# Moving eight weight buffers by 64 bytes within a 128-byte line of on-chip memory, in a float32 transformer kernel

## The chip, the core and the metric

The kernel runs on one core of one Trainium2 chip. The metric is the device time of one execution in microseconds (us). TensorE is the matmul engine (PE in the profile, and PEld for its loads of the stationary operand), VectorE is DVE, ScalarE is ACT, GpSimd is POOL, and SyncE is SP, which issues the DMAs. SBUF is the on-chip memory from which the engines read (128 partitions; an address here is a byte offset within a partition, the same in all of them), and PSUM is the memory that TensorE writes.

## The reference, cut to what matters

Two residual-network blocks run after one another over 256 tokens of width 1024: projections, a gated convolution, memory attention, stick-breaking attention, gated linear attention, spatial gating, and three gated feed-forward networks. Nearly all the work is in products of the form

```python
h = rmsnorm(x, gain)                                   # (256, 1024)
p = h @ w                                              # every projection, w is (1024, n)
x = x + (act(h @ w_gate) * (h @ w_up)) @ w_down        # three times, 2816 wide
```

All inputs and outputs are float32, and the products are asked for at float32 accuracy.

## The kernel before, in words

**Weights.** The weights are cut into 356 slots of 128 x 1024 float32 (512 KB each), which pass through the kernel in one fixed order (`STAGES`, line 41). With 48 more pieces for the modulation vectors they form one stream of 404 loads. SP loads them one after another into six buffers `raw0` to `raw5` (line 350), and waits before each load until the buffer's last reader is done (line 349).

**Halves.** TensorE reads a faster float32 format (fp32r) that holds fewer bits, so each weight is split into a high and a low part, and so is each activation. For slot n, ACT copies `raw` into `w_hi[n % 4]` in that format (line 886), and DVE subtracts: `w_lo[n % 4] = raw - w_hi[n % 4]` (line 1408; in the third feed-forward network POOL does about every second one, line 2108). Four buffers of each kind form the ring (`RING = 4`). ACT waits at line 885 until TensorE has used the slot four earlier.

**Matmuls.** A product is made of three: high x high, high x low and low x high (`mm3`, lines 378 to 381). A call `pe.matmul(o, w, x)` loads `w` as the stationary operand, 128 columns that stay in the array (the profile shows this as LDWEIGHTS), and streams `x`, the moving operand, past it. The load for the next matmul runs while the present one streams. There are two kinds of slot:
- `tall` (line 390) and `down` (line 519): 8 chunks x 3 matmuls. Stationary is a 128-column chunk of `w_hi` or `w_lo`; moving are 256 tokens of an activation (`H`, `Y`, `CX`, `HP`, or `G` in `down`). 24 matmuls a slot.
- `wide` (line 401), called for the value projections by `project_tokens`: the other way round. Stationary are 128 tokens of an activation, moving are 512 or 256 columns of `w_hi` or `w_lo`.

```python
def mm3(o, wh, wl, xh, xl, start, stop):                                              # 378
    pe.matmul(o, wh, xh, start=start, stop=False, skip_group_check=True)              # 379
    pe.matmul(o, wh, xl, start=False, stop=False, skip_group_check=True)              # 380
    return pe.matmul(o, wl, xh, start=False, stop=stop, skip_group_check=True)        # 381
```

Products that are not of weights (attention, sums over partitions, transposes) go through `mm` (line 384) as plain float32 and read no weight half.

**Order.** Each engine has a program written out by hand (`pe_program`, `act_program`, `dve_program`, `pool_program`, `sync_program`). Side tasks such as attention are put between slots by generators (`Side`, `Pace`). The engines meet only at semaphores (`mark`, `past`).

**Places in SBUF.** `sb(...)` allocates tensors in the order of the calls from line 214 on, each start rounded up to 32 bytes. The compiled program of before has them at these places:

| tensors | first start (bytes) | start modulo 128 |
|---|---|---|
| `raw0` to `raw5` | 1152 | 0 |
| `w_hi0` to `w_hi3` | 25728 | 0 |
| `w_lo0` to `w_lo3` | 42112 | 0 |
| `X`, `H_hi`, `H_lo`, `Y_hi`, `Y_lo`, `SQ`, `RS` | 58496 | 0 |
| `G_hi0` to `G_lo1`, `GF`, `consts` | 109696 | 0 |
| `CROW` | 120992 | 32 |
| `ARENA` and its areas of whole kilobytes | 129472 | 64 |
| `CX_lo`, `CX_hi` (activations of the context) | 191424 | 64 |
| `HP` (rows of 258 elements) | 207808 | 64, and 8 bytes on for each chunk |

A chunk of a weight half is 512 bytes long and one of `H`, `Y` or `CX` 1024 bytes, so every chunk of one tensor begins at the same place modulo 128. The one exception is `HP`, whose chunks are 1032 bytes apart.

Of the kernel before, what the change touches and what calls it, by code (L numbers as in the profile page):

```python
# [8 lines left out]
P = 128  # L9
# [17 lines left out]
STACK = 96  # L27
EPS = 1e-6
RING = 4
RAW = 6  # L30

F32 = mybir.dt.float32
# [3 lines left out]
ALU = mybir.AluOpType  # L36
AX = mybir.AxisListType.X

# [15 lines left out]
for _l, _j in ((_l, _j) for _l in range(2) for _j in range(FC)):  # L54
# [4 lines left out]
    MOD_ORDER += _now  # L59
    MODS_AFTER[AT[f"ffn{_l}"] + (RING + 1 + 2 * _j if _j < 2 else RING + 3 * _j)] = _now  # L60
assert MOD_ORDER == list(range(NMOD))
# [17 lines left out]
def raw_of(kind, n):  # L79
    return LOAD_OF[kind, n] % RAW  # L80

# [42 lines left out]
class Signals:  # L124
# [14 lines left out]
    def mark(self, name, *index, by=1):  # L139
        sem = SEMAPHORE.get(name, name)  # L140
        self.count[sem] = self.count.get(sem, 0) + by
        assert (name, *index) not in self.value, (name, index)
        self.value[(name, *index)] = self.count[sem]
        return self.sem(name), by

    def past(self, name, *index):
        return self.sem(name), self.table[(name, *index)] if self.table else 1
# [43 lines left out]
def lo_by(n):  # L191
    first = AT["ffn2"] + RING
    return "lo_pool" if n >= first and (n % 2 or n == first) else "lo_dve"
# [6 lines left out]
def freed(i):  # L200
    kind, n = LOADS[i]
    return (lo_by(n), n) if kind == "slot" else ("mod_dot", n, 0)


def build(nc, table, stream, vec, xT, memT, ctxT, c_rows, sq_consts, masks, scan_mask, sgu_bc, sgu_wT, gla_w2, out):
    pe, act, dve, pool, sp = nc.tensor, nc.scalar, nc.vector, nc.gpsimd, nc.sync
    with ExitStack() as ctx:
        def sb(name, shape, dt=F32):
            return ctx.enter_context(nc.sbuf_tensor(name, shape, dt))
# [2 lines left out]
        mark, past = signals.mark, signals.past  # L212

        raw = [sb(f"raw{r}", [P, D]) for r in range(RAW)]
        w_hi = [sb(f"w_hi{r}", [P, D], F32R) for r in range(RING)]
        w_lo = [sb(f"w_lo{r}", [P, D], F32R) for r in range(RING)]
        X = sb("X", [P, KC, T])
        H = (sb("H_hi", [P, KC, T], F32R), sb("H_lo", [P, KC, T], F32R))
        Y = (sb("Y_hi", [P, KC, T], F32R), sb("Y_lo", [P, KC, T], F32R))
# [123 lines left out]
        def sync_program():  # L343
# [3 lines left out]
            for i, (kind, n) in enumerate(LOADS):  # L347
                if i >= RAW:
                    sp.wait_ge(*past(*freed(i - RAW)))
                sp.dma_start(raw[i % RAW][:], stream[i]).then_inc(*mark(f"loaded{i % RAW}", kind, n, by=16))  # L350
                if (kind, n) == ("slot", 0):
                    sp.dma_start(MEM[:, 4:8], memT[:, 4:8]).then_inc(*mark("mem_half1", by=16))
                if (kind, n) == ("slot", 1):
                    sp.dma_start(X[:], xT).then_inc(*mark("x_in", by=16))
                if (kind, n) == ("slot", AT["a_c"]):
# [13 lines left out]
        def pe_program():  # L369
# [16 lines left out]
            def slot():  # L386
                pe.wait_ge(*past(lo_by(n), n))
                return n % RING

# [482 lines left out]
        def act_program():  # L872
# [5 lines left out]
            def fill():  # L878
                nonlocal n
                if n >= N_SLOTS:  # L880
                    return
                at = raw_of("slot", n)
                act.wait_ge(*past(f"loaded{at}", "slot", n))
                if n >= RING:
                    act.wait_ge(*past("used", n - RING))
                act.activation(w_hi[n % RING][:], raw[at][:], ACT.Copy).then_inc(*mark("hi", n))  # L886
                n += 1

            def squares(tag, src, ready, at=SQ):
                for c in range(0, KC, 2):  # L890
                    if ready:
                        act.wait_ge(*past(*ready[c // 2]))
                    act.activation(at[:, c:c + 2], src[:, c:c + 2], ACT.Square).then_inc(*mark("sq", tag, c // 2))
# [103 lines left out]
            def residual_square(l, into=None, g=None):  # L997
                def then(i):
                    act.wait_ge(*past("added", l, i))
                    act.activation(SQ[:, i], X[:, i], ACT.Square).then_inc(*mark("res_sq", l, i))  # L1000
                    if into is not None:
                        act.activation(into[0][:, i, 0:T], X[:, i], ACT.Copy,
                                       scale=g(i)).then_inc(*mark("h_hi", l, i))
# [77 lines left out]
            def block1_end():  # L1081
                pace = Pace()
                squares("final", X, [("x_add", 1, c) for c in range(KC // 2)])
                yield from pace.to(4)
# [141 lines left out]
            act.wait_ge(*past("x_in"))  # L1226
            squares("mix0", X, None, CSQ)
            fill()
# [1072 lines left out]
```

## Time and profile before

| | |
|---|---|
| three runs | 1151.97, 1153.01 and 1153.58 us; median 1153.01 |
| the profiled execution | 1151.95 us, of which the span from the first to the last instruction is 1150.6 us |
| granted TensorE clock | 0.995 of full speed |
| DMA | 221.49 MB, mean 192 GB/s |

A row of the profile names the source line, the engine, the operation, the output and inputs (buffer numbers left out), the shape, and the count. After the bar stand the busy time in us and the mean duration of one in ns, and after a second bar the engine's idle time ahead of these instructions, with what ended most of it. Matmuls overlap, so the duration of one is not the pace: the pace is read from start to start. The busy share of PE says little for the same reason.

### The profile page before, as it was taken

To read this page: it belongs to the slowest core of one execution; us is meant where nothing else is said; L and a number is where in the kernel's file an instruction comes from. 1 tells how busy PE (TensorE), PEld (TensorE's weight loads), DVE (VectorE), ACT (ScalarE), POOL (GpSimd) and SP (SyncE) were. 2 spreads that over 40 slices of the span, in tenths; PEclk is the share of its full clock that TensorE was granted. 3 is DMA by queue.
4 is the path that set the end of the run, shared out by engine and by line. 5 is a ranking of instruction groups with operands and counts; after the bars stand their busy time and mean duration, and the time that the engine had idled before them with its cause. 6 is when DMAs were issued, how large, how long until landed. Compare 5 with 4: busy or idle time off the path is not lost.

```text
span 1150.6 us, 21726 instructions
## 1 busy us (share of the span) xinstructions
PE 1124.2 (98%) x8918; PEld 1085.8 (94%) x8918; DVE 837.2 (73%) x1304; ACT 627.7 (55%) x951; POOL 146.2 (13%) x109
## 2 busy tenths in 40 slices
PE   7999999999999999999999999999999998999997
PEld 6989999999998899999999888989999998999996
DVE  5767687888876766777777677497646788767766
ACT  5655644434665655444444675676547465455553
POOL 0002201000000003000000000000000044344441
PEclk9999999999999999999999999999999999999999
DMA  8655578776644345788888655354435544555640
GB/s 324 220 160 171 177 234 282 240 252 208 200 132 150 125 140 191 247 272 276 270 263 285 235 165 183 110 183 155 140 123 172 183 165 129 192 182 177 191 158 37
DMA packets 60322, 221.49 MB, mean 192 GB/s; under 512 B 6720, under 2 KB 6976, under 8 KB 59840
## 3 DMA queue, kind: packets, MB, share of 16 engines
q1 hardware_dynamic: 59760, 218.53, 58.5%
q8 instruction: 71, 1.16, 0.4%
q10 hardware_dynamic: 288, 1.05, 0.2%
q0 software_dynamic: 176, 0.52, 0.1%
q14 instruction: 27, 0.22, 0.1%
HBM read 219.03 MB, written 1.05 MB: 191 GB/s over the span
## 4 chain that ended last, share of the span: by engine, by line
PE 83%; DVE 11%; ACT 4%; issue 2%; DMA 1%; SPq 0%; ACTq 0%; DVEq 0%
PE PS L379 23%; PE PS L380 23%; PE PS L381 23%; PE PS L384 13%; DVE w_lo L1408 3%; ACT w_hi L886 2%; DVE PS L2053 2%; DVE ARENA L1441 1%; DMA ARENA<-memT 1%; DVE SQ L1441 0%; DVE SQ L1716 0%; DVE H_lo L1451 0%; ACT ARENA L983 0%; DVE Y_lo L1451 0%; DVE Y_lo L1447 0%
## 5 line engine op out<-in xcount | busy, mean ns | idle before, releaser
L1408 DVE TENSOR_TENSOR w_lo<-raw,w_hi 128x1024 fp32r<-128x1024 f32 x324 | 396.9, 1228 | 164.6 <-ACT w_hi L886 164.0
L886 ACT ACTIVATE w_hi<-raw 128x1024 fp32r<-128x1024 f32 x356 | 371.6, 1054 | 133.4 <-PE PS L381 107.6
L379 PE MATMUL PS<-Y_hi,w_hi 128*128 128x256 f32 x1208 | 347.0, 287 | 9.5 <-DVE Y_lo L1447 3.4
L380 PE MATMUL PS<-Y_lo,w_hi 128*128 128x256 f32 x1208 | 343.0, 284 | 0.0
L381 PE MATMUL PS<-Y_hi,w_lo 128*128 128x256 f32 x1208 | 342.9, 284 | 0.0
L379 PEld LDWEIGHTS PS<-Y_hi,w_hi 128*128 128x128 f32 x1208 | 232.6, 193 | 13.7 <-issue 4.3
L380 PEld LDWEIGHTS PS<-Y_lo,w_hi 128*128 128x128 f32 x1208 | 232.8, 193 | 0.5 <-issue 0.2
L381 PEld LDWEIGHTS PS<-Y_hi,w_lo 128*128 128x128 f32 x1208 | 232.8, 193 | 0.0
L379 PE MATMUL PS<-H_hi,w_hi 128*128 128x256 f32 x768 | 220.1, 287 | 1.7 <-DVE w_lo L1408 0.9
L380 PE MATMUL PS<-H_lo,w_hi 128*128 128x256 f32 x768 | 217.3, 283 | 0.0
L381 PE MATMUL PS<-H_hi,w_lo 128*128 128x256 f32 x768 | 217.2, 283 | 0.0
L379 PEld LDWEIGHTS PS<-H_hi,w_hi 128*128 128x128 f32 x768 | 147.1, 192 | 6.4 <-issue 3.0
L379 PE MATMUL PS<-G_hi,w_hi 128*128 128x256 f32 x528 | 149.6, 283 | 1.9 <-DVE G_lo L1539 1.9
L380 PE MATMUL PS<-G_lo,w_hi 128*128 128x256 f32 x528 | 149.4, 283 | 0.0
L381 PE MATMUL PS<-G_hi,w_lo 128*128 128x256 f32 x528 | 149.4, 283 | 0.0
L380 PEld LDWEIGHTS PS<-H_lo,w_hi 128*128 128x128 f32 x768 | 147.2, 192 | 0.1
L381 PEld LDWEIGHTS PS<-H_hi,w_lo 128*128 128x128 f32 x768 | 147.2, 192 | 0.0
L379 PEld LDWEIGHTS PS<-G_hi,w_hi 128*128 128x128 f32 x528 | 101.4, 192 | 2.3 <-issue 2.3
L380 PEld LDWEIGHTS PS<-G_lo,w_hi 128*128 128x128 f32 x528 | 101.4, 192 | 0.0
L381 PEld LDWEIGHTS PS<-G_hi,w_lo 128*128 128x128 f32 x528 | 101.4, 192 | 0.0
L1028 ACT ACTIVATE GF<-GF 128x256 f32<-128x256 f32 x44 | 18.4, 418 | 140.0 <-DVE GF L1550 140.0
L2108 POOL TENSOR_TENSOR w_lo<-raw,w_hi 128x1024 fp32r<-128x1024 f32 x32 | 77.8, 2433 | 113.0 <-ACT w_hi L886 113.0
(251 smaller groups left out, 1392.1 us busy)
## 6 DMA issues: line engine op xcount, KB each, us to landing
raw<-stream SPq DMA_DIRECT2D x404, 512.0 KB, 4.1
ARENA<-memT SPq DMA_DIRECT2D x2, 512.0 KB, 7.6
X<-xT SPq DMA_DIRECT2D x1, 1024.0 KB, 11.2
ARENA<-ctxT SPq DMA_DIRECT2D x1, 1024.0 KB, 5.3
ARENA<-memT SPq DMA_DIRECT2D x1, 1024.0 KB, 9.4
outT<-ARENA SPq DMA_DIRECT2D x2, 512.0 KB, 2.6
CROW<-c_rows SPq DMA_DIRECT2D x1, 512.0 KB, 10.2
ARENA<-c_rows SPq DMA_DIRECT2D x1, 512.0 KB, 12.3
```

Of the source, the lines that this page charges most:

```text
L379: pe.matmul(o, wh, xh, start=start, stop=False, skip_group_check=True)
L380: pe.matmul(o, wh, xl, start=False, stop=False, skip_group_check=True)
L381: return pe.matmul(o, wl, xh, start=False, stop=stop, skip_group_check=True)
L384: return pe.matmul(o, w, x, start=start, stop=stop, skip_group_check=True)
L886: act.activation(w_hi[n % RING][:], raw[at][:], ACT.Copy).then_inc(*mark("hi", n))
L1028: act.activation(GF[:], GF[:], ACT.Silu).then_inc(*mark("silu", l, j))
L1408: dve.tensor_tensor(w_lo[n % RING][:], raw[raw_of("slot", n)][:], w_hi[n % RING][:], ALU.subtract).then_inc(*mark("lo_dve", n))
L1441: dve.scalar_tensor_tensor(via[:, c], src[:, c], g(c), rs[1], ALU.mult, ALU.mult).then_inc(*mark("norm", tag, c))
L2053: dve.scalar_tensor_tensor(conv_sum(j), IMGS[:, j % 2, r0:r0 + ROWS, c0:c0 + COLS], gain("fconv", j + t * FC), conv_sum(j), ALU.mult, ALU. ...
L2108: pool.tensor_tensor(w_lo[n % RING][:], raw[raw_of("slot", n)][:], w_hi[n % RING][:], ALU.subtract).then_inc(*mark("lo_pool", n))
```

## The change

Two unused tensors of 16 float32 a partition (64 bytes) are allocated: one ahead of the weight halves, one behind them. The eight weight halves so begin 64 bytes later (25792 and 42176, modulo 128: 64), and everything behind them 128 bytes later, at the same place modulo 128 as before. The raw buffers lie ahead of both and do not move. No instruction is added, removed or reordered.

```diff
+HALF_LINE = 16
 ...
         raw = [sb(f"raw{r}", [P, D]) for r in range(RAW)]
+        sb("phase", [P, HALF_LINE])
         w_hi = [sb(f"w_hi{r}", [P, D], F32R) for r in range(RING)]
         w_lo = [sb(f"w_lo{r}", [P, D], F32R) for r in range(RING)]
+        sb("whole", [P, HALF_LINE])
         X = sb("X", [P, KC, T])
```

## Rows read from the trace of the kernel before

**Rows 1.** The page: busy time, share of the span, instructions of each engine
```profile
PE 1124.2 (98%) x8918; PEld 1085.8 (94%) x8918; DVE 837.2 (73%) x1304; ACT 627.7 (55%) x951; POOL 146.2 (13%) x109
```

**Rows 2.** The page: the chain of waits that ended last, by engine
```profile
PE 83%; DVE 11%; ACT 4%; issue 2%; DMA 1%; SPq 0%; ACTq 0%; DVEq 0%
```

**Rows 3.** Groups by line and shape: matmuls with a weight half, tall kinds
```profile
L379 PE MATMUL PS<-Y_hi,w_hi 128*128 128x256 f32 x1208 | 347.0, 287 | 9.5 <-DVE Y_lo L1447 3.4 <-DVE w_lo L1408 3.2 <-DVE G_lo L1539 2.7
...
L379 PE MATMUL PS<-H_hi,w_hi 128*128 128x256 f32 x768 | 220.1, 287 | 1.7 <-DVE w_lo L1408 0.9 <-DVE H_lo L1626 0.2
...
L379 PE MATMUL PS<-G_hi,w_hi 128*128 128x256 f32 x528 | 149.6, 283 | 1.9 <-DVE G_lo L1539 1.9
...
L379 PE MATMUL PS<-CX_hi,w_hi 128*128 128x256 f32 x40 | 11.5, 287 | 0.0
...
L379 PE MATMUL PS<-HP,w_hi 128*128 128x258 f32 x32 | 9.4, 292 | 0.0
```

**Rows 4.** Stretches: us, each engine's busy time (instructions), granted clock, DMA share, GB/s
```profile
870.00:939.00 69.00, 69.00 (x578) 69.00 (x577) 54.69 (x80) 39.11 (x55) 7.96 (x6) 1.00 0.59 189
1000.00:1120.00 120.00, 120.00 (x1002) 120.00 (x1001) 88.15 (x160) 61.40 (x98) 50.48 (x21) 1.00 0.57 181
460.00:640.00 180.00, 180.00 (x1503) 180.00 (x1502) 135.18 (x198) 80.06 (x109) 15.77 (x22) 1.00 0.83 270
...
140.00:305.00 165.00, 164.62 (x1373) 164.44 (x1372) 134.11 (x208) 77.36 (x111) 13.55 (x19) 1.00 0.75 238
```

**Rows 5.** PE in order of time (start, duration), tall slot with CX, 14 matmuls
```profile
412.33 0.28 PE L380 MATMUL PS<-CX_lo,w_hi 128*128 128x256 f32 x1
...
413.86 0.28 PE L381 MATMUL PS<-CX_hi,w_lo 128*128 128x256 f32 x1
```

**Rows 6.** PE in order of time, tall slot with Y just begun, 13 matmuls
```profile
668.16 0.28 PE L379 MATMUL PS<-Y_hi,w_hi 128*128 128x256 f32 x1
...
669.58 0.28 PE L379 MATMUL PS<-Y_hi,w_hi 128*128 128x256 f32 x1
```

**Rows 7.** PE in order of time, wide slot with Y: first, 7th, 24th matmul
```profile
751.95 0.40 PE L384 MATMUL PS<-w_hi,Y_hi 128*128 128x512 f32 x1
...
753.34 0.39 PE L384 MATMUL PS<-w_hi,Y_hi 128*128 128x512 f32 x1
...
757.19 0.39 PE L384 MATMUL PS<-w_lo,Y_hi 128*128 128x512 f32 x1
```

**Rows 8.** PE in order of time, wide slot with CX, 13 matmuls
```profile
645.10 0.39 PE L384 MATMUL PS<-w_hi,CX_hi 128*128 128x512 f32 x1
...
647.90 0.39 PE L384 MATMUL PS<-w_hi,CX_hi 128*128 128x512 f32 x1
```

**Rows 9.** PE in order of time, slot with HP (258 moving columns), 21 matmuls
```profile
939.46 0.28 PE L379 MATMUL PS<-HP,w_hi 128*128 128x258 f32 x1
...
941.86 0.28 PE L381 MATMUL PS<-HP,w_lo 128*128 128x258 f32 x1
```

**Rows 10.** Groups by line and shape: wide matmuls with a weight half
```profile
L384 PE MATMUL PS<-w_hi,Y_hi 128*128 128x512 f32 x80 | 32.5, 406 | 0.0
...
L384 PE MATMUL PS<-w_hi,Y_hi 128*128 128x256 f32 x48 | 14.3, 298 | 0.0
...
L384 PE MATMUL PS<-w_hi,CX_hi 128*128 128x512 f32 x32 | 13.0, 405 | 0.0
```

**Rows 11.** Groups by line: DVE and ACT instructions that touch raw or a weight half
```profile
L1408 DVE TENSOR_TENSOR w_lo<-raw,w_hi 128x1024 fp32r<-128x1024 f32 x324 | 396.9, 1228 | 164.6 <-ACT w_hi L886 164.0
L886 ACT ACTIVATE w_hi<-raw 128x1024 fp32r<-128x1024 f32 x356 | 371.6, 1054 | 133.4 <-PE PS L381 107.6 <-PE PS L384 25.7
...
L1427 DVE SCALAR_TENSOR_TENSOR raw<-raw,CROW 128x1024 f32<-128x1024 f32 x48 | 57.9, 1221 | 0.6
...
L1423 DVE SCALAR_TENSOR_TENSOR SQ<-raw,ARENA 128x1024 f32<-128x1024 f32 x16 | 19.5, 1219 | 0.0
```

**Rows 12.** One line's instructions: minimum, median and maximum duration in ns
```profile
L1408 DVE TENSOR_TENSOR w_lo<-raw,w_hi x324: 1172/1224/2048, 11.2 to 1126.9; 128x1024 fp32r<-128x1024 f32 x162
```

## The prediction

> **What bounds the kernel now.** I read the busy times first: PE is busy for 98% of the span, DVE for 73%, ACT for 55% [rows 1]. The chain of waits agrees, with PE holding 83% of it and DVE 11% [rows 2]. But overlapping matmuls make a PE look busy whatever its pace, so I turned to stretches of time and counted matmuls. In three long stretches every matmul is a tall one with a weight half, and the counts (two or three of which were already running when the stretch began) give one and the same pace: 69.00 us over 575, 120.00 us over 1000, 180.00 us over 1500, each 120.0 ns from start to start [rows 4]. The clock is 1.00 of full speed, 2.4 GHz, throughout, so 256 columns at one a cycle would take 106.7 ns; 13.3 ns of each matmul are something else. DVE in these stretches is busy for 54.69 of 69, 88.15 of 120 and 135.18 of 180 us, and ACT for less [rows 4]: nobody else sets the pace. The question is therefore only whether a different place of the weights changes these 13.3 ns.
>
> **What the trace says about places.** Before, stationary weights and moving `H`, `Y`, `G` all begin at 0 modulo 128. Only `CX` begins at 64, so its rows show what a distance of 64 does, while weights are still at 0. In a tall slot with `CX` 13 intervals take 413.86 - 412.33 = 1.53 us, 117.7 ns each [rows 5], against 120.0. That is 2.3 ns less per matmul. In the wide slots, where the roles are exchanged, the same distance goes the other way: with `CX` 12 intervals take 2.80 us, 233.3 ns each [rows 8]; with `Y` the first 6 intervals take 1.39 us, 231.7 ns each, and the 17 after them 3.85 us, 226.5 ns each [rows 7]. A tall slot with `Y` that has just begun shows the same transition: its first 12 intervals take 1.42 us, 118.3 ns each [rows 6], then comes the 120.0.
>
> I read this as one mechanism. The load of the next stationary operand reads SBUF while the moving operand is read. Where both streams begin at the same place modulo 128, they fall into a fixed step with each other a few matmuls after any pause: 120.0 ns in tall slots, 226.5 in wide ones. At a distance of 64 they never fall into it, and the pace stays near that of the first matmuls: 117.7 and 233.3. What speaks for the distance rather than for the place of one operand is that `Y`, with both operands at 0, runs the first matmuls at nearly the `CX` paces. Distances are what the change exchanges: weights against `H`, `Y`, `G` go from 0 to 64, weights against `CX` from 64 to 0.
>
> **The sum, by parts.**
> Tall matmuls with `Y`, `H` and `G`: three groups of 1208, 768 and 528 at line 379 [rows 3], each as often again at lines 380 and 381, so 2504 x 3 = 7512. At 2.3 ns each: -17.3 us. Some come right behind a pause and run at 118 already [rows 6]; I take 5% off, an estimate: -16.4 us.
> Tall matmuls with `CX`: 40 x 3 = 120 [rows 3], which go from 117.7 to 120.0: +0.3 us.
> `HP`: 32 x 3 = 96 matmuls of 258 columns [rows 3]. Its chunks begin at places 8 bytes apart, so its distances are mixed before and after. Its pace is 2.40 us over 20, 120.0 ns [rows 9], of which two more columns are 0.8. Between 0 and 2.3 ns each way, 0.2 us at most: taken as 0.
> Wide matmuls with `Y`, 512 columns: 80 x 3 = 240 [rows 10], from 226.5 to 233.3, +6.8 ns: +1.6 us. Those with `CX`: 32 x 3 = 96 [rows 10], the other way: -0.7 us. Those with 256 columns: 48 x 3 = 144 [rows 10], which have the shape of tall ones: -0.3 us.
> TensorE together: -16.4 + 0.3 + 1.6 - 0.7 - 0.3 = -15.5 us.
>
> DVE at line 1408 now reads `raw` at 0 and `w_hi` at 64. It has 1228 ns with both at 0. Similar instructions of the same size with unequal places are line 1427 (0 and 32) at 1221 ns, and line 1423 (0 and 64) at 1219 ns [rows 11]. The nearest rows say up to 9 ns less; from above the bound is its own slowest, 2048 ns [rows 12]. I take no change. Nine ns over 324 would be 2.9 us of DVE's time, beside 1150.6 - 837.2 = 313 us in which it idles [rows 1]. ACT at line 886, 1054 ns [rows 11], writes at 64 where it wrote at 0. No row shows that copy at unequal places, so it is bounded by DVE's differences, 1% either way. It idles for 45% of the span. POOL idles for 87%. The DMAs write `raw`, which does not move, so they cost what they cost now. Other matmuls read no weight half: nothing.
>
> What covers these engines shrinks a little. In the stretch where DVE is fullest it is busy for 134.11 of 165 us [rows 4]. Were this stretch 2% shorter, DVE would be at 83% of it: still no bound. The DMA engines are at 0.83 in the second feed-forward network with 270 GB/s [rows 4], and would be asked for 275 GB/s. Some of PE's 26 idle us (1150.6 - 1124.2) [rows 1] end with DVE or ACT work that had fallen behind earlier; there a faster PE only waits longer. I give back 0.5 us for it. So -15.0 us.
>
> The profiled execution took 1151.95 us (span 1150.6 and 1.35 around it), so it would become 1137.0. It lies 1.1 us under the median of the runs, 1153.0, and the same difference gives a median of **1138.0 us**, 1.3% less. For the size alone: with the first-matmul pace of 118.3 instead of 117.7 the gain at 7512 is 12.8 us before corrections, and the result 1142; if the distance cost nothing extra beyond a pace of 117.0, 3.0 ns each, it would be 1132.
>
> **A rule that speaks against it.** The rows show two paces for the same instruction. The Trainium skill, in "TensorE: Matmul & The Clock Gate", section "Part 2: What happens when you issue a matmul", says that TensorE has two independent read ports of SBUF, and that loading the next weights doesn't take bandwidth from the running matmul. By that rule the place of either operand would be indifferent and the time would stay 1153.0. Of itself the trace doesn't agree, 117.7 against 120.0 ns, unless something else in the stretch of `CX` made the difference; that is the first rival.
>
> **Rivals.**
> *No change.* The two paces are not of the distance but of what else ran: at 408 to 428 us the other engines and the DMAs may just have been quieter. Then every tall matmul keeps 120.0, and the time is 1153.0. Against it: stretches with DMA shares of 0.57, 0.59 and 0.83 all have exactly 120.0 [rows 4], and the CX pace differs in the wide slots too, in the other direction. Chance 0.09.
> *Slower: the stationary operand's own place costs.* In the wide slots with `CX` the stationary operand is what lies at 64, and they are slower by 6.8 ns than with `Y` [rows 7, 8]. In the tall slots with `CX` the moving operand lies at 64, and they are faster. After the change the weights, stationary in tall slots, lie at 64 and the moving operand at 0. If a stationary start at 64 costs by itself, tall matmuls pay up to 6.8 ns: 7512 x 6.8 = 51 us, giving 1204. It turns the sign from the point where that cost exceeds the 2.3 ns of the distance. Against it: wide slots with `Y`, stationary at 0, run their first matmuls at 231.7 [rows 7], so 1.6 of the 6.8 at most are the place's own, which over 7512 would be 12 us against the 17.3. Chance 0.06.
> *Half the gain.* The pace falls, but with weights at 64 the streams fall into a step of another length, or DVE or ACT work that was covered comes out behind each stage: about 1145.5. Chance 0.08.
>
> **How the numbers follow.** The forecast, the distance with its full effect, has 0.77, and its own range is 1132 to 1143 from the two sizes above. Half the gain makes 0.85 for faster; no change 0.09; slower 0.06. 0.2%, 2.3 us, is about what a measurement of this kernel can tell from no change. The range runs from 1132 to 1148: it takes in the forecast's own range and most of the half gain, and leaves out no change and slower.
>
> **What would show it.** Right: stretches in the feed-forward networks with 1500 tall matmuls in about 176.6 us instead of 180.00; tall slots with `CX` at 120.0; wide slots with `Y` that stay near 233, and with `CX` that fall to 226.5; DVE's line 1408 within 1% of 1228 ns. Wrong: 120.0 ns again with `H` and `Y` (no change), or above 120 (slower), or a PE that pauses in front of slots for `w_lo` where it didn't (half).

## The result, and the profile after

The changed kernel takes 1140.98 us (median of 4 runs, 1139.28 to 1141.62), the kernel before 1153.03 us. The ratio is 0.9894 with a 95% interval of 0.9877 to 0.9911: faster by 1.1%. The forecast was 1138.0 us, in a range of 1132 to 1148. The profiled execution took 1140.45 us against 1151.95, which is 11.5 us less where the sum gave 15.0.

Line numbers of the changed kernel are three higher than before. First the page: the busy times and the clock in 40 slices, which answer to [rows 1].

```profile
PE 1112.7 (98%) x8918; PEld 1071.7 (94%) x8918; DVE 836.9 (73%) x1304; ACT 627.6 (55%) x951; POOL 146.2 (13%) x109
...
PEclk9999999999999999999999999999999998999999
```

The other engines did the same work in the same time: DVE is busy for 836.9 us against 837.2. The groups by line and shape, which answer to [rows 11], say so one by one.

```profile
L1411 DVE TENSOR_TENSOR w_lo<-raw,w_hi 128x1024 fp32r<-128x1024 f32 x324 | 397.0, 1228 | 159.9 <-ACT w_hi L889 159.2
L889 ACT ACTIVATE w_hi<-raw 128x1024 fp32r<-128x1024 f32 x356 | 371.6, 1054 | 129.7 <-PE PS L384 103.8 <-PE PS L387 25.8
```

DVE's 1228 ns and ACT's 1054 ns are those of before to the nanosecond, although each of these instructions now has `raw` at 0 and a weight half at 64.

The pace of the matmuls, in stretches that hold only tall slots (us, busy times with counts for PE, PEld, DVE, ACT and POOL, granted clock, DMA share, GB/s), answers to [rows 4].

```profile
460.00:620.00 160.00, 160.00 (x1361) 160.00 (x1360) 122.44 (x182) 71.77 (x99) 14.84 (x20) 1.00 0.86 281
1000.00:1110.00 110.00, 110.00 (x936) 110.00 (x935) 81.02 (x148) 57.86 (x91) 48.04 (x20) 1.00 0.57 181
```

Of each count three are matmuls that were already running when the stretch began. So 160.00 us over 1358 is 117.8 ns each, and 110.00 over 933 is 117.9: the pace that `CX` had before, 2.2 ns less than the 120.0 of [rows 4]. The clock is 1.00 in both.

The wide slots with `Y`, in order of time (start, duration), answer to [rows 7].

```profile
743.66 0.39 PE L387 MATMUL PS<-w_hi,Y_hi 128*128 128x512 f32 x1
...
749.03 0.40 PE L387 MATMUL PS<-w_lo,Y_hi 128*128 128x512 f32 x1
```

23 intervals take 5.37 us, 233.5 ns each, and they no longer settle at 226.5. That is the loss that was forecast. `CX` did something else than forecast, in a tall slot and in a wide one:

```profile
407.12 0.28 PE L382 MATMUL PS<-CX_hi,w_hi 128*128 128x256 f32 x1
...
409.50 0.28 PE L384 MATMUL PS<-CX_hi,w_lo 128*128 128x256 f32 x1
```

```profile
636.78 0.40 PE L387 MATMUL PS<-w_lo,CX_hi 128*128 128x512 f32 x1
...
640.03 0.40 PE L387 MATMUL PS<-w_hi,CX_lo 128*128 128x512 f32 x1
```

The first is 2.38 us over 20 intervals, 119.0 ns, the second 3.25 us over 14, 232.1 ns. With both operands at 64 modulo 128 they should have settled at 120.0 and 226.5, and did neither. Modulo 256, `CX` now lies 128 bytes from the weights, while `H` and `Y` had lain at 0. That was the first sign that the period is longer than 128 bytes.

**Where the missing microseconds are.** The clock row of the page has an 8 in one slice. The stretches around it:

```profile
944.70:951.50 6.80, 6.50 (x26) 6.11 (x27) 6.62 (x16) 4.71 (x9) 1.42 (x1) 0.50 0.00 0
972.00:975.40 3.40, 3.40 (x18) 3.40 (x17) 3.19 (x7) 0.55 (x1) 0.00 (x0) 0.50 0.97 358
```

In these 10.2 us the granted clock was 0.50, 1.2 GHz, each time behind a pause of PE of more than 2 us (2.48 and 2.44 us from the last matmul's end). The kernel before makes the same two pauses and lost the clock only behind the first, for 3.4 us. Its stretches behind the two pauses:

```profile
951.00:962.00 11.00, 7.88 (x44) 6.79 (x44) 9.40 (x23) 7.75 (x15) 2.20 (x2) 0.84 0.23 76
...
980.70:988.00 7.30, 7.28 (x60) 7.28 (x61) 5.65 (x12) 2.40 (x3) 2.42 (x1) 1.00 0.63 218
```

In the second of the half-clock stretches of the changed kernel 16 new matmuls take 3.40 us, 213 ns each instead of 118: 1.5 us lost there alone. Near the start it was the other way round: the kernel before ran at half clock from 13.1 to 16.5 us, and the changed kernel at full clock there.

```profile
13.10:16.50 3.40, 3.40 (x18) 3.40 (x18) 3.40 (x7) 2.32 (x5) 1.44 (x3) 0.50 1.02 413
```

### The profile page after: what moved, and what is told of

The parts are those of the page before. It is cut to its first block, busy times and chain, and to the rows that moved or that the text cites. A ratio compares the mean times of both kernels' runs of the same rounds, so it can differ in the third digit from the quotient of the medians.

```text
span 1139.1 us, 21726 instructions
## 1 busy us (share of the span) xinstructions
PE 1112.7 (98%) x8918; PEld 1071.7 (94%) x8918; DVE 836.9 (73%) x1304; ACT 627.6 (55%) x951; POOL 146.2 (13%) x109
## 4 chain that ended last, share of the span: by engine, by line
PE 83%; DVE 11%; ACT 4%; issue 2%; DMA 1%; SPq 0%; ACTq 0%; DVEq 0%
PE PS L382 23%; PE PS L384 23%; PE PS L383 23%; PE PS L387 13%; DVE w_lo L1411 3%; ACT w_hi L889 2%; DVE PS L2056 2%; DVE ARENA L1444 1%; DMA ARENA<-memT 1%; DVE SQ L1444 0%; DVE SQ L1719 0%; DVE H_lo L1454 0%; ACT ARENA L986 0%; DVE Y_lo L1454 0%; DVE Y_lo L1450 0%
## 5 line engine op out<-in xcount | busy, mean ns | idle before, releaser
L1411 DVE TENSOR_TENSOR w_lo<-raw,w_hi 128x1024 fp32r<-128x1024 f32 x324 | 397.0, 1228 | 159.9 <-ACT w_hi L889 159.2
L889 ACT ACTIVATE w_hi<-raw 128x1024 fp32r<-128x1024 f32 x356 | 371.6, 1054 | 129.7 <-PE PS L384 103.8
L382 PE MATMUL PS<-Y_hi,w_hi 128*128 128x256 f32 x1208 | 343.3, 284 | 7.9 <-DVE Y_lo L1450 3.4
L384 PE MATMUL PS<-Y_hi,w_lo 128*128 128x256 f32 x1208 | 339.3, 281 | 0.0
L383 PE MATMUL PS<-Y_lo,w_hi 128*128 128x256 f32 x1208 | 339.0, 281 | 0.0
L382 PEld LDWEIGHTS PS<-Y_hi,w_hi 128*128 128x128 f32 x1208 | 227.9, 189 | 11.8 <-issue 4.1
L383 PEld LDWEIGHTS PS<-Y_lo,w_hi 128*128 128x128 f32 x1208 | 228.6, 189 | 0.5 <-issue 0.2
L384 PEld LDWEIGHTS PS<-Y_hi,w_lo 128*128 128x128 f32 x1208 | 228.5, 189 | 0.0
L383 PE MATMUL PS<-H_lo,w_hi 128*128 128x256 f32 x768 | 214.3, 279 | 0.0
L382 PEld LDWEIGHTS PS<-H_hi,w_hi 128*128 128x128 f32 x768 | 143.8, 187 | 7.3 <-issue 3.5
L383 PEld LDWEIGHTS PS<-H_lo,w_hi 128*128 128x128 f32 x768 | 144.2, 188 | 0.1
L384 PEld LDWEIGHTS PS<-H_hi,w_lo 128*128 128x128 f32 x768 | 144.2, 188 | 0.0
```

What stands on the lines that cost most here:

```text
L1411: dve.tensor_tensor(w_lo[n % RING][:], raw[raw_of("slot", n)][:], w_hi[n % RING][:], ALU.subtract).then_inc(*mark("lo_dve", n))
```

## The experiments

In the runs below only the places of tensors differ, except where filler matmuls, which compute nothing that is kept, are named. "Distance" is the start of `H`, `Y` and `G` minus the start of the weight halves, modulo 256 bytes. The distance of `CX` is always 64 more. The distance was 0 before and is 64 after the change.

### Place or distance

Activations and all behind them 64 bytes further, the weights where they were (run at 64, roles exchanged):

```diff
         w_lo = [sb(f"w_lo{r}", [P, D], F32R) for r in range(RING)]
+        sb("whole", [P, 16])
         X = sb("X", [P, KC, T])
```

> Weights stay at 0 modulo 128, X, H, Y, G and all behind them begin at 64: the distance of 64 of the change, with the two operands' places exchanged. Theory (the distance decides): 1500 tall matmuls of the second feed-forward network take 176.6 us (117.7 ns each) as in the changed kernel, the time is about 1141 us. Rival (the place of the stationary operand decides): weights are where they were before, so 120.0 ns and 1153 us.

It took 1139.95 us (4 runs, 1138.55 to 1142.45), ratio 0.9885 [0.9868, 0.9902], and the same count of matmuls in the same stretch as the changed kernel, 117.8 ns each:

```profile
460.00:620.00 160.00, 160.00 (x1361) 160.00 (x1360) 122.44 (x182) 72.17 (x99) 14.81 (x20) 1.00 0.85 281
```

Weights and all behind them at 64, so that the weights lie as in the changed kernel and the distance is 0:

```diff
         raw = [sb(f"raw{r}", [P, D]) for r in range(RAW)]
+        sb("phase", [P, 16])
         w_hi = [sb(f"w_hi{r}", [P, D], F32R) for r in range(RING)]
```

> Weights at 64 modulo 128 and everything behind them at 64 too: the weights lie as in the changed kernel, but the distance to H, Y and G is 0 again. Theory (distance): 120.0 ns, 1153 us. Rival (place of the weights): 117.7 ns, 1141 us.

It took 1152.86 us (10 runs), ratio 0.9994 [0.9984, 1.0004]:

```profile
460.00:620.00 160.00, 160.00 (x1336) 160.00 (x1335) 121.03 (x178) 71.34 (x97) 14.13 (x20) 1.00 0.82 269
```

160.00 us over 1333 is 120.0 ns. The two runs settle it from both sides: the distance gives the gain, with either operand displaced, and the displaced weights alone give nothing. The rival by which the stationary operand's own place costs falls with them. They show that the distance is the cause of the gain, and not by what mechanism: that the load of the next stationary operand gets in the way of the moving one is the prediction's reading, and no run here took the loads away.

### The period, and other distances

The pad behind the weights was 32, 128, 160 and 256 bytes, with no pad ahead of them. For 48 and 16 bytes, where the allocation's steps of 32 are too coarse, the halves are slices of one tensor that is 256 bytes longer and begin 52 elements, 208 bytes, into it (for 16, offset 60 in place of 52):

```diff
-        w_hi = [sb(f"w_hi{r}", [P, D], F32R) for r in range(RING)]
-        w_lo = [sb(f"w_lo{r}", [P, D], F32R) for r in range(RING)]
+        halves = sb("halves_ring", [P, 2 * RING * D + 64], F32R)
+        w_hi = [halves[:, 52 + r * D:52 + (r + 1) * D] for r in range(RING)]
+        w_lo = [halves[:, 52 + (RING + r) * D:52 + (RING + r + 1) * D] for r in range(RING)]
```

> Weights stay, all behind them 32 bytes further. Theory (distance, and anything but equal places avoids the fixed step): 117.7 ns in tall slots, about 1141 us. If the two streams must be a half line apart: between 117.7 and 120.0, 1141 to 1153 us.

> Weights stay, all behind them 128 bytes further, so the distance is 0 modulo 128 and 128 modulo 256. If the distance counts modulo 128: 120.0 ns in tall slots and 226.5 ns in wide ones with Y, 1153 us. If it counts over more than 128 bytes, as CX in the changed kernel hints (now 128 apart modulo 256, and neither at 120.0 nor at 226.5): about 118.9 ns and 232.9 ns, and 1146 us.

> Weights stay, all behind them 160 bytes further; CX then lies 224 bytes from the weights modulo 256. Both distances are new. If the pace is a function of the distance modulo 256 without symmetry, anything from 116.7 to 120.0 ns in tall slots, 1136 to 1153 us. If it depended only on whether the distance is below or above half a period, it would be near the 117.0 ns that CX had at 192, and about 1139 us.

> Weights stay, all behind them 256 bytes further. Theory (the distance counts modulo 256): as before, 120.0 ns in the tall slots, 226.5 ns in settled wide ones with Y, CX at 117.8, 1153 us. Rival (a longer period, or any displacement from the start helps): below 120.0 ns.

> The weight halves are slices of one tensor that begin 208 bytes into it, so H, Y and G are 48 bytes from them modulo 256, and CX 112. Theory (a smooth function of the distance modulo 256): between the 116.7 ns at 32 and the 117.8 at 64, about 117.2 ns, 1138 us. Rival (every step of 16 bytes has its own pattern): outside that interval.

> As the run at 48, with slices that begin 240 bytes in: H, Y and G are 16 bytes from the weights, CX 80. Theory (smooth): between 120.0 at 0 and 116.7 at 32, about 118.3 ns, 1144 us. Rival (only exactly equal places fall into the fixed step): 116.7 ns or less, 1136 us.

| distance | time, us (runs) | ratio, 95% interval | second network, ns a matmul | third network, ns a matmul |
|---|---|---|---|---|
| 256, that is 0 | 1152.75 (8) | 1.0002 [0.9991, 1.0013] | 120.1 | 120.1 |
| 16 | 1144.64 (7; 1139.53 to 1148.28) | 0.9921 [0.9894, 0.9948] | 120.0 | 117.4 |
| 32 | 1136.67 (2) | 0.9854 [0.9834, 0.9874] | 116.7 | 116.8 |
| 48 | 1137.09 (2; 1134.43 and 1139.75) | 0.9865 [0.9807, 0.9922] | 116.7 | 120.1 |
| 64 (changed kernel) | 1140.98 (4) | 0.9894 [0.9877, 0.9911] | 117.8 | 117.9 |
| 128 | 1147.33 (2) | 0.9947 [0.9926, 0.9968] | 118.7 | 118.7 |
| 160 | 1143.00 (2) | 0.9916 [0.9887, 0.9945] | 117.4 | 117.4 |

The last two columns are each worked out as above, from the stretches 460 to 620 us and 1000 to 1110 us. At a distance of 256 the first row is that of distance 0 again:

```profile
460.00:620.00 160.00, 160.00 (x1335) 160.00 (x1335) 121.20 (x178) 71.35 (x97) 14.10 (x19) 1.00 0.82 269
```

and at 128 it is not:

```profile
460.00:620.00 160.00, 160.00 (x1351) 160.00 (x1350) 122.14 (x179) 72.29 (x99) 14.02 (x19) 1.00 0.83 273
```

So 256 acts as 0 and 128 does not: the distance counts modulo 256. The forecast's 128 was wrong, and that is why `CX` did not settle. The traces agree by all slots together: with `H`, `Y` and `G` at 128 the mean intervals are 118.7 ns (tall) and 232.3 (wide), and for `CX` in the changed kernel, which lies at 128 too, 118.6 and 232.4. No run shows a line of memory of 128 bytes, of which the title and the change speak; already 16 bytes change the paces.

At 32 the forecast was 117.7 ns and 1141 us, and both came out lower; at 160 the narrower forecast, near 117.0 ns and 1139 us, came out at 117.4 and 1143.00. The expectation of one smooth pace for each distance falls as well. At 16 and at 48 the two networks of one execution run at different paces. Distance 48:

```profile
460.00:620.00 160.00, 160.00 (x1374) 160.00 (x1373) 123.85 (x184) 72.83 (x100) 14.79 (x20) 1.00 0.86 284
1000.00:1110.00 110.00, 110.00 (x919) 110.00 (x918) 79.06 (x143) 56.60 (x89) 45.52 (x19) 1.00 0.55 178
```

110.00 us over 916 is the old 120.1 ns, and the second network, with the same operands at the same distance, had 116.7. At distance 16 it is the other way round:

```profile
460.00:620.00 160.00, 160.00 (x1336) 160.00 (x1335) 121.24 (x177) 71.25 (x98) 14.08 (x19) 1.00 0.84 272
1000.00:1110.00 110.00, 110.00 (x940) 110.00 (x939) 83.44 (x154) 58.11 (x92) 46.98 (x20) 1.00 0.58 188
```

The medians at 16 and 48, 1144.64 and 1137.09 us, do lie at the smooth forecasts of 1144 and 1138, but as averages of two paces: that agreement is luck. The distance does not set one pace: different distances show different sets of paces. In every trace an unbroken stretch of more than 200 tall matmuls keeps one pace from its first few dozen on, for up to 187 us, and another pace is found only behind an interruption, which can be short: in the filled kernel at 64, below, it goes from 113.3 to 117.8 ns at 451 to 452 us, where the starts lie at most 0.4 us apart and one plain float32 matmul comes between. The times of the runs fit that: 8.8 us lie between the fastest and the slowest run at distance 16, against 2.3 us between those of the changed kernel.

### The clock behind the pauses

Plain float32 matmuls were put into the three longest pauses of PE behind the start, at 305, 941 and 968 us in the changed kernel. `nil` is a small tensor that DVE sets to zero. The first two groups go to free PSUM banks; the third multiplies by zeros and is added to bank 4, which leaves its contents as they are.

```diff
                 down(l, FC - 2)
+                if l == 0:
+                    claim(0)
+                    for _ in range(8):
+                        mm(PS[:, 0, 0:T], ONES, consts[:, 0:T])
                 down(l, FC - 1)
 ...
                 emptied[2 * p] = [("gelu", j)]
+                if j == 4:
+                    pe.wait_ge(*past("nil"))
+                    for _ in range(11):
+                        mm(PS[0:32, 4, 0:T], nil[:], consts[:, 0:T], False, False)
                 claim(2 * p + 1)
 ...
+            claim(7)
+            for _ in range(11):
+                mm(PS[:, 7, 0:T], ONES, consts[:, 0:T])
             for j in range(LEAD, FC):
```

> The changed kernel, with 8, 11 and 11 plain float32 matmuls put into the three pauses of PE over 2 us (ahead of the last down slot of the first feed-forward network, ahead of the slot that waits for norm2, and ahead of the up slot of round 4 of the third network). They compute nothing that is kept. Theory (the missing 3 us of the forecast were lost to the half clock behind these pauses): the 10 us at half clock between 940 and 976 us go, the time is about 1138 us. Rival (the saved time went into longer waits for DVE): the clock stays full and the time stays within 1 us of 1141.

> The kernel before with the same 30 matmuls in its pauses. Theory: it loses only the one stretch of 3.4 us at half clock that it had, so about 1152 us, and the difference to the filled changed kernel is 14 to 15 us instead of 12. Rival: the difference stays 12 us.

> Distance 32 with the same matmuls in the pauses. With 116.7 ns a tall matmul and the clock kept: 1133 to 1134 us, below every kernel so far.

> Distance 32 alone once more. If its 116.7 ns are what this distance always gives: 1136 to 1137 us in every run. If more than one step is possible at this distance, as at 16 and 48, some runs come out at 1140 us or more.

| kernel | time, us (runs) | ratio, 95% interval | profiled execution, us | clock |
|---|---|---|---|---|
| distance 64, filled | 1135.51 (5; 1133.77 to 1141.11) | 0.9862 [0.9839, 0.9885] | 1141.11 | 0.998 |
| distance 0, filled | 1155.05 (11; 1154.19 to 1156.81) | 1.0020 [1.0011, 1.0029] | 1155.58 | 0.997 |
| distance 32, filled | 1137.72 (4; 1136.05 to 1140.15) | 0.9873 [0.9856, 0.9889] | 1140.15 | 0.996 |
| distance 32 again | 1139.03 (5; 1133.18 to 1139.70) | 0.9871 [0.9851, 0.9890] | 1137.10 | 0.993 |

The fillers kept the clock. The same stretch with them (filled, distance 64) and without (the changed kernel):

```profile
941.00:952.00 11.00, 10.62 (x67) 9.44 (x66) 9.42 (x22) 7.55 (x15) 2.21 (x2) 1.00 0.21 73
```

```profile
941.00:952.00 11.00, 8.08 (x39) 7.30 (x38) 9.41 (x22) 7.49 (x15) 2.21 (x2) 0.69 0.22 72
```

1.00 against 0.69. But I had sized them wrongly. A float32 matmul was taken for one record of 0.22 us, and it is two, as PE in order of time shows for 11 of them at distance 64:

```profile
941.39 4.91 PE L388 MATMUL PS<-consts 128*128 128x256 f32 x22
...
945.95 0.47 PE L383 MATMUL PS<-Y_hi,w_hi 128*128 128x256 f32 x1
```

They take 4.6 us up to the next matmul, in a pause that had been 2.8. At distance 0, where there was little clock to win, they cost 2.5 us by the medians (1155.05 against the 1152.54 of the kernel before beside them). The comparison that stands is filled against filled, both at full clock in the networks. The profiled executions differ by 1155.58 - 1141.11 = 14.5 us, as the theory had it, where unfilled ones differ by 11.5. But not all of these 3.0 us are the clock's. The third network, where the half clock lay, takes 199.7 us against 202.5 by the starts of its matmuls, 2.9 less, where unfilled it is 1.2 less: the clock gives back 1.7 us. The rest is a lower pace in parts of this one execution, shown next: over all tall matmuls the mean interval is 117.5 ns instead of 117.75, which is 1.7 us over 7512, and small waits take some of it back. The medians differ by 19.5 us, more than the theory allows. The profiled execution at distance 64 was the slowest of its five; three others took 1133.77 to 1135.51 us at the same mean clock of 0.997 or 0.998. What they did is not in a trace. The profiled one gives a hint, in the output projection of the second layer:

```profile
429.00:444.00 15.00, 15.00 (x135) 15.00 (x134) 12.16 (x16) 9.64 (x16) 5.84 (x4) 1.00 0.62 204
```

The changed kernel has 130 records there, at the same distance:

```profile
429.00:444.00 15.00, 15.00 (x130) 15.00 (x129) 12.09 (x16) 9.70 (x17) 5.85 (x4) 1.00 0.57 181
```

15.00 us over 132 is 113.6 ns, against 118.1 over 127: a lower pace than any tall one so far. The changed kernel has that pace too, in the wide matmuls of 256 columns with `Y` of the second layer:

```profile
317.72 0.28 PE L387 MATMUL PS<-w_hi,Y_hi 128*128 128x256 f32 x1
...
322.14 0.28 PE L387 MATMUL PS<-w_hi,Y_hi 128*128 128x256 f32 x1
```

These are 39 intervals in 4.42 us, 113.3 ns each. One whole network of 1584 matmuls at 4.5 ns less would be 7.1 us, about the 7.3 us between 1141.11 and 1133.77. That fits, and isn't shown. Nor does the profiled execution alone decide between the two expectations for this run: its 1141.11 us is the rival's time, at the clock of the theory, and the median, 1135.51, is below both.

At distance 32, repeated, the expectation of one pace in every run falls. The profiled execution has two paces:

```profile
130.00:260.00 130.00, 130.00 (x1116) 130.00 (x1116) 105.65 (x156) 62.97 (x86) 11.84 (x16) 1.00 0.78 255
460.00:620.00 160.00, 160.00 (x1361) 160.00 (x1360) 122.65 (x181) 72.48 (x99) 14.89 (x20) 1.00 0.85 281
```

The first network runs at 130.00/1113 = 116.8 ns and the second at 117.8. In the first run at this distance it was the reverse, the second at 116.7 and the first at 130.00/1103 = 117.9. All seven unfilled runs at distance 32 lie between 1133.18 and 1139.70 us, the four of the changed kernel between 1139.28 and 1141.62. The intervals of the ratios, 0.9851 to 0.9890 and 0.9877 to 0.9911, still overlap, so distance 32 is likely better than the change by some 2 or 3 us, and that isn't settled. The filled kernel at 64 has the lowest median, 1135.51 us, but its interval overlaps the change's too. The fillers at 32 missed their forecast of 1133 to 1134 us: the median is 1137.72, and in the profiled execution the second network is at 117.8 ns again. All versions at 32 and 64 are clear of the kernel before.

The clock itself also differs between executions of one program. Around the pause at 305 us it was at 0.50 from 306.5 to 309.9 us in the first profiled execution at distance 32, with a pause of 2.23 us, and stayed at 1.00 in the second, with one of 2.23 us too. At 48, 128 and 160 it fell there as well, for 3.4 us each, and at 0 and 64 it did not.

## Why the prediction was right, and what it got wrong

**The main step held.** Tall matmuls went from 120.0 to 117.8 ns, where 117.7 was forecast from 13 intervals of `CX`. Over all of them, matmuls right behind pauses included, the mean interval in the trace went from 119.94 to 117.75 ns: 7512 x 2.19 = 16.5 us, where the sum had 16.4. That it is the distance that matters, not the place of one operand, was forecast and is shown by the two runs above.

**The small terms.** Wide matmuls with `Y`: mean interval 228.5 to 233.4 ns, 240 x 4.9 = +1.2 us (forecast +1.6, because I took all of them as settled at 226.5 before). Wide ones of 256 columns: 119.6 to 115.0, 144 x 4.6 = -0.7 us (forecast -0.3). `CX` failed in its mechanism: tall +0.1 us and wide -0.1 us, where +0.3 and -0.7 were forecast. The step "weights against `CX` from 64 to 0" took the period for 128; it is 256, and `CX` went from 64 to 128. `HP` stayed within 0.1 us. The upper end of the forecast's own range is given as 1143 where the size it is taken from gives 1142; nothing hangs on it. Together -16.5 + 0.1 + 1.2 - 0.1 - 0.7 = -16.0 us, against the -15.5 of the sum.

**The picture behind the number.** The prediction said that at a distance of 64 the streams never fall into a fixed step and stay at the pace of the first matmuls. The runs show otherwise: 117.8 ns is itself a held pace, over 1559 matmuls in a row from 452.0 to 635.6 us, as 120.0 was before, and 113.3 ns was seen at this distance too. The number was right because it was read from `CX`, which lay at 64. That one pace then held in all longer stretches of tall slots was luck: at 16, 32, 48, 128 and 160 it changed between stretches of one execution.

**The step that was mis-sized** is the one that gave back 0.5 us for everything that happens between matmuls. It was 16.0 - 11.5 = 4.5 us in the profiled execution. By the starts of the matmuls in the traces, the second network takes 187.2 us instead of 190.6, 3.4 less, as the pace says. The first takes 190.6 instead of 193.0, only 2.4 less: its two waits for DVE, at 278 and 305 us, grew from 0.66 and 1.80 to 1.20 and 2.27 us, 1.0 us together. The third takes 199.24 instead of 200.47, only 1.2 less, though its 1488 tall matmuls with `Y` and `G` should save 3.3: here the clock was at half for 10.2 us instead of 3.4. At the start nothing was lost in the end: the first weight matmul came at 13.0 instead of 12.5 us, but the kernel before then had its half clock from 13.1 to 16.5 us, and the matmul on `RS` that follows starts at 22.06 us instead of 22.10. About 1.5 us is spread over small waits, and I did not follow it. I had looked at what covers PE when it gets faster, and not at what the clock does when the same pauses fall elsewhere.

**The rivals.** No change: excluded by the time and by the pace, at DMA shares from 0.57 to 0.86. Behind it stood what the Trainium skill says in "TensorE: Matmul & The Clock Gate", section "Part 2: What happens when you issue a matmul", that loading the next weights takes nothing from the running matmul. That the places are therefore indifferent does not hold in this case, by 120.0 against 117.8 ns with only the addresses changed; whether it is the load that interferes was not isolated. Slower: excluded. Half the gain: its second branch, covered work that comes out, is real and took 1 us of 16; its first, a fixed step of another length, is what exists at every distance, the changed one included, where it is short enough to give the full gain.

## What to carry to other kernels

Where TensorE is the bound and its matmuls are short, count them over a stretch at full clock and compare the pace with the columns: here 13 of 120 ns were more than the 256 columns take at 2.4 GHz, 2 to 7 of them depended on the distance of the two operands, and a pad of 32 or 64 bytes between the weight buffers and the activations took 1 to 1.5% off the whole kernel. Choose the distance modulo 256 by trying a few, and look at every long stretch of each trace and at more than one run, since one distance can hold two paces. When the matmuls get faster, the pauses between them stay, so read the granted clock behind each pause before believing the sum.

## What was not expected of the hardware

- The stream of matmuls locks into one of a few paces and can keep it over a whole network: 113.3 (seen only over shorter stretches), 116.7, 117.4, 117.8, 118.7 and 120.0 ns for 256 columns at 2.4 GHz. The last is 288 cycles, 32 more than the columns, and a settled wide matmul at distance 0, 226.5 ns, is 544 cycles, again 32 more than its 512. A stationary chunk of 512 bytes is 32 lines of 16 bytes, the line size that the Trainium skill gives in "SBUF — State Buffer", section "Specifications (TRN2)". That each line of the load costs the moving stream one cycle at distance 0 is a guess from these numbers. No run isolates it.
- At distances 16, 32, 48, 128 and 160 two paces or more were seen in one execution (at 160, 870 to 929 us ran at 120 ns; at 128, 789 to 806 us did), at 64 in the filled kernel, and in the four traces at 0 and 256 no settled pace but 120.0. Which one holds differs between executions: at 32 the first network had 117.9 ns in one and 116.8 in the other. The spread from 1139.53 to 1148.28 us at distance 16 for the same program fits that. What decides it at a restart was not found.
- DVE and ACT did not care. DVE's subtraction took 1228 ns and ACT's copy 1054 ns with their operands at equal places and at places 64 bytes apart modulo 128.
